# The first panels of a two-layer hybrid kernel: turned rows of x from the host, sums of squares on GpSimd

## What is computed

```python
h = rms_norm(x, g_mix);  proj = h @ w_in               # x: 256 x 1024, w_in: 1024 x 8,000 or so
kv_m = rms_norm(mem, g_mem) @ w_mem_kv                 # mem: 256 x 1024
# rms_norm(t, g) = t * rsqrt(mean(t * t, axis=-1) + 1e-6) * g
```

## Time and profile before

| | |
|---|---|
| median of three runs | 929.32 us (929.22 to 929.41) |
| span of the profiled execution | 926.1 us; the profile gives no other time for that execution |
| TensorE busy | 905.7 us, 98% of the span |
| VectorE, ScalarE, GpSimd busy | 720.6, 534.9, 161.8 us |
| mean granted TensorE clock | 0.997 of full speed |

### The profile page before, as it was taken

How to read it: one execution, slowest core, us unless ns; L and a number is a source line. 1 busy time by engine, 2 the same in 40 slices (tenths; PEclk the granted TensorE clock), 3 DMA queues, 4 the chain that set the end, 5 groups by cost and what they waited for, 6 DMA issues and landing times.

```text
span 926.1 us, 13743 instructions
## 1 busy us (share of the span) xinstructions
PE 905.7 (98%) x4668; PEld 730.1 (79%) x4668; DVE 720.6 (78%) x1030; ACT 534.9 (58%) x831; POOL 161.8 (17%) x247
## 2 busy tenths in 40 slices
PE   8999999999999999999999999999999999999996
PEld 7888888777878778888888887666678788888885
DVE  4779476878777778887679788865668879999976
ACT  6775754476775575555333345656664676666633
POOL 7000000216500000110112001550000023444400
PEclk9999999999999999999999999999999999999998
DMA  9746744876552447887598755322245566555572
GB/s 319 204 150 208 269 138 133 285 263 196 178 191 96 138 141 253 270 266 251 171 358 304 254 159 183 117 78 80 92 131 183 155 191 179 169 176 177 172 251 78
DMA packets 100534, 176.16 MB, mean 190 GB/s; under 512 B 8560, under 2 KB 36592, under 8 KB 100352
## 3 DMA queue, kind: packets, MB, share of 16 engines
q1 hardware_dynamic: 93120, 149.87, 50.7%
q0 software_dynamic: 7184, 25.50, 8.2%
q10 hardware_dynamic: 176, 0.08, 0.0%
HBM read 174.38 MB, written 1.05 MB: 189 GB/s over the span
## 4 chain that ended last, share of the span: by engine, by line
PE 59%; DVE 4%; ACT 2%; issue 1%; DVEq 0%
PE acc L775 50%; PE turned L1251 2%; PE scores L1240 1%; PE turned L867 1%; DVE wlo L1938 1%; PE turned L1353 1%; PE turned L1140 1%; PE turned L1163 1%; PE turned L811 1%; ACT prob L1790 0%; DVE soft L2643 0%; ACT whi L1393 0%; DVE turn L2025 0%; PE turned L1255 0%; ACT turn L1847 0%
## 5 line engine op out<-in xcount | busy, mean ns | idle before, releaser
L1938 DVE TENSOR_TENSOR wlo<-raw,whi 128x1024 fp32r<-128x1024 f32 (+3 forms) x269 | 346.6, 1308 | 81.8 <-ACT whi L1393 71.2
L1393 ACT CAST whi<-raw 128x1024 fp32r<-128x1024 f32 (+3 forms) x269 | 273.3, 1032 | 161.7 <-PE acc L775 118.0
L775 PE MATMUL acc<-whi,lta_hi 128*128 128x512 f32 (+2 forms) x576 | 163.4, 399 | 0.2 <-DVEq L2515 0.2
L775 PE MATMUL acc<-whi,lta_lo 128*128 128x512 f32 (+2 forms) x576 | 155.8, 385 | 0.0
L775 PE MATMUL acc<-wlo,lta_hi 128*128 128x512 f32 (+2 forms) x576 | 155.4, 385 | 0.0
L775 PEld LDWEIGHTS acc<-whi,lta_hi 128*128 128x128 f32 x576 | 101.1, 188 | 30.8 <-issue 10.8
L775 PEld LDWEIGHTS acc<-whi,lta_lo 128*128 128x128 f32 x576 | 106.9, 188 | 22.4
L775 PEld LDWEIGHTS acc<-wlo,lta_hi 128*128 128x128 f32 x576 | 106.9, 188 | 21.9
L657 POOL DMA_DIRECT2D wm<-in_w_mod x48 | 34.4, 719 | 428.6 <-DVEq L2069 245.6
L775 PE MATMUL acc<-whi,ltb_hi 128*128 128x512 f32 (+1 forms) x268 | 73.3, 392 | 1.6 <-ACT ltb_hi L1851 0.8
L775 PE MATMUL acc<-wlo,ltb_hi 128*128 128x512 f32 (+1 forms) x268 | 71.1, 384 | 1.6 <-DVE wlo L1938 1.6
(11 more groups left out here) (371 smaller groups left out, 1301.7 us busy)
## 6 DMA issues: line engine op xcount, KB each, us to landing
raw<-in_w_in SPq DMA_DIRECT2D x88, 512.0 KB, 4.2
wm<-in_w_mod POOLq DMA_DIRECT2D x48, 512.0 KB, 5.5
raw<-in_w_up SPq DMA_DIRECT2D x88, 256.0 KB, 3.1
raw<-in_w_up SPq DMA_DIRECT2D x32, 512.0 KB, 4.6
raw<-in_w_down SPq DMA_DIRECT2D x32, 512.0 KB, 5.2
raw<-in_w_down SPq DMA_DIRECT2D x44, 256.0 KB, 3.0
raw<-in_w_o SPq DMA_DIRECT2D x8, 512.0 KB, 4.5
raw<-in_w_out SPq DMA_DIRECT2D x8, 512.0 KB, 4.6
```

The lines of the kernel that those rows point to most:

```text
L775: ins = pe.matmul(acc[s][:, t, 0:n], lhs[part][:, kt0 + kk, tok], w[:, u % RING, kk, 0:n], start=(opens and k == 0 and kk == 0 and j == 0) ...
L1393: act.copy(whi[:, s, :, 0:n], raw[:, s, :, 0:n]).then_inc(hi_ready, 1)
L1938: dve.tensor_tensor(wlo[:, s, :, 0:n], raw[:, s, :, 0:n], whi[:, s, :, 0:n].bitcast(F32), ALU.subtract)\
```

## The change

The host hands over x turned as well (`x_t`), the eight gains in one array and AQ's two column ranges side by side (`w_aq`). In the kernel:

- SyncE loads a quarter of `xT` behind each unit of MK2. Memory's rows aren't loaded; x's rows (for the residual) follow the first two units of V0.
- `lta` is made of `xT` in SBUF with the gain and without the root. TensorE turns nothing here. ScalarE applies the root of x as it evicts AQ, GQ, CK, GK, V0, V1 and the Q panels, in two instructions in place of one; VectorE does so for R and the gates.
- GpSimd squares `memT` and then `xT`, 512 columns at a time, and adds them up: eight squares, six additions and two last additions of 256 columns. TensorE sums over the partitions with two matmuls of one column for each of the two (`row_sums`), memory's after MK2's first unit, x's after AQ. VectorE's `row_var` and the root follow.
- The first half of unit 0 is cast by VectorE. The table of the root is loaded at the start.

```diff
-    out += [("AQ", KT, 2)]
+    out += [("AQ", KT, 1)]
...
-    out = g("h", 4) + ["aT", "z.0", "z.1", "mqT", "mkT", "ck"]
+    out = ["mem_sum", "x_sum", "aT", "z.0", "z.1", "mqT", "mkT", "ck"]
...
+        feature_squares = [prob[:, 0, 0:SEQ], prob[:, 1, 0:SEQ]]
...
-                return [(0, rows(w, k)[:, :, COL["a"]:COL["a"] + GATE_RANK]),
-                        (GATE_RANK, rows(w, k)[:, :, COL["qm"]:COL["qm"] + 256])]
+                return [(0, a["w_aq"][:, UNIT * k:UNIT * k + UNIT, :])]
...
-                    if name == "MK1" and k == units_of(name) - 1:
-                        for t in range(T):
-                            sp.dma_start(memx[:, t], a["mem"][t * P:(t + 1) * P, :]).then_inc(ev(f"mem{t}_landed"), 16)
-                    if name == "MK2" and k < T:
-                        sp.dma_start(x[:, k], a["x"][k * P:(k + 1) * P, :]).then_inc(ev(f"x{k}_landed"), 16)
+                    if name == "MK2":
+                        sp.dma_start(xT[:, 2 * k:2 * k + 2, :], a["x_t"][:, 2 * k:2 * k + 2, :])\
+                          .then_inc(ev(f"xT{k}_landed"), 16)
+                    if name == "V0" and k < T:
+                        sp.dma_start(x[:, k], a["x"][k * P:(k + 1) * P, :]).then_inc(ev("x_landed"), 16)
...
+            for s, (name, src, landed_as) in enumerate((("mem", memT, "memT"), ("x", xT, "xT"))):
+                total, part = work[:, s, 0:COLS], work[:, s, COLS:D]
+                for g in range(4):
+                    pool.wait_ge(ev(f"{landed_as}{g}_landed"), 16)
+                    v = src[:, 2 * g:2 * g + 2, :].rearrange("p a b -> p (a b)")
+                    order.done(pool.tensor_tensor(part if g else total, v, v, ALU.mult))
+                    if g:
+                        order.done(pool.tensor_tensor(total, total, part, ALU.add))
+                pool.tensor_tensor(feature_squares[s], total[:, 0:SEQ], total[:, SEQ:COLS], ALU.add)\
+                    .then_inc(ev(f"{name}_squares"), 1)
...
-            for name, view in GAIN.items():
-                pool.dma_start(view, a[name].partition_broadcast(P)).then_inc(ev("gains_landed"), 16)
+            pool.dma_start(gains[:], a["gains"].partition_broadcast(P)).then_inc(ev("gains_landed"), 16)
...
+            def row_sums(name, squares):
+                bank, full = t_begin(f"{name}_sum")
+                pe.wait_ge(ev(f"{name}_squares"), 1)
+                for t in range(T):
+                    ins = pe.matmul(bank[:, t:t + 1], squares[:, P * t:P * t + P], one_col[:], start=True, stop=True)
+                ins.then_inc(full, 1)
+
             for k in range(4):
-                if k == 3:
-                    pe.wait_ge(ev("h_scaled"), T)
-                    turn_tokens("h", work, groups=(0, 1))
                 unit("MK2", k, ltb)
-            turn_tokens("h", work, groups=(2, 3))
+                if k == 0:
+                    row_sums("mem", feature_squares[0])
             panel("AQ", lta, NARROW["AQ"], new="h")
+            row_sums("x", feature_squares[1])
...
-            for name, src, s in (("me", memx, 0), ("h", x[:], 1)):
-                for t in range(T):
-                    ...
-                    act.activation(prob[:].rearrange("p a b -> p (a b)"), src[:, t, :], ACT.Square,
-                                   accum_out=stat[:, s, t:t + 1]).then_inc(ev(f"{name}_sum"), 1)
...
+            for g in range(4):
+                ahead(2 + g)
+                lt_act("h", lta, (g,))
+            ahead(PLAN.unit["AQ"] - 2)
+            sqrt("mem", stat[:, 0, 2:4])
...
-            evac("AQ", aq[:], NARROW["AQ"])
+            ahead(last_unit("AQ") + 1)
+            sqrt("x", stat[:, 1, 2:4])
+            normed_rows("AQ", aq, NARROW["AQ"])
...
+            dve.wait_ge(ev("first_landed"), 16)
+            dve.tensor_copy(whi[:, 0, 0], raw[:, 0, 0]).then_inc(ev("first_hi"), 1)
             lt_dve("me", ltb, col("g_mem", 0, 8), between=lambda g: ahead(g - 2), sent=memT)
...
-            for t in range(T):
-                dve.tensor_scalar(work[:, t], x[:, t], stat[:, 1, 2 + t:3 + t], None, ALU.mult)\
-                   .then_inc(ev("h_scaled"), 1)
...
+            for g in range(4):
+                ahead(2 + g)
+                lt_dve("h", lta, col("g_mix", 0, 8), groups=(g,))
+            ahead(PLAN.unit["AQ"] - 2)
+            row_var("mem", 0)
+            inverse("mem", stat[:, 0, 2:4])
+            dve.sem_inc(ev("mem_inverse"), 1)
+            ahead(PLAN.unit["GQ"])
+            row_var("x", 1)
+            inverse("x", stat[:, 1, 2:4])
+            dve.sem_inc(ev("x_inverse"), 1)
+            evacuated("AQ")
```

More of the change, by code:

```diff
@@ L289, in hybrid_kernel @@
         ln_sums = sb("ln_sums", [P, T, 8])
-        gains = sb("gains", [P, 6 * 64 + DV_GLA + HEADS])
+        gains = sb("gains", [P, sum(n for _, n in GAINS)])
         ROWS, at = {}, 0
@@ L584, in _ @@
                     panel(name)
-                if name == "MK2":
+                if name == "AQ":
                     sp.dma_start(ccol[:], a["columns"][:, 96:96 + 8 * FT2].rearrange("p (v r) -> p v r", v=4))\
@@ L1418, in lt_act @@
                     if name in LT_DIRECT:
-                        if name == "me":
-                            act.wait_ge(ev(f"memT{g}_landed"), 16)
+                        if name in LT_HOST:
+                            act.wait_ge(ev(f"{'memT' if name == 'me' else 'xT'}{g}_landed"), 16)
                         else:
@@ L1531, in _, with normed_rows @@
             normed_memory("MK1", kvm[:, :, 256:768], COLS)
[L1532 to L1535, removed]
             normed_memory("MK2", kvm[:, :, 768:1280], COLS)
-            evac("AQ", aq[:], NARROW["AQ"])
+            ahead(last_unit("AQ") + 1)
+            sqrt("x", stat[:, 1, 2:4])
+            def normed_rows(name, dst, n=COLS):
+                ahead(last_unit(name) + 1)
+                panel_wait(name)
+                if name == "AQ":
+                    act.wait_ge(ev("x_inverse"), 1)
+                s, _ = PLAN.bank(name)
+                for t in range(T):
+                    ins = act.activation(dst[:, t], acc[s][:, t, 0:n], ACT.Copy, scale=stat[:, 1, 2 + t:3 + t])
+                ins.then_inc(panel_out[s], 1)
+            normed_rows("AQ", aq, NARROW["AQ"])
             act.dma_start(wg[0:GATE_RANK, :], a["w_gla_gate"]).then_inc(ev("wg_landed"), 16)
@@ L1581, in mem_after @@
                         act.wait_ge(panel_out[b], k + 2)
-                    act.activation(rsig, acc[PLAN.bank(name)[0]][:], ACT.Sigmoid).then_inc(ev("r_sig"), 1)
+                    for t in range(T):
+                        ins = act.activation(rsig[:, t], acc[PLAN.bank(name)[0]][:, t], ACT.Sigmoid,
+                                             scale=stat[:, 1, 2 + t:3 + t])
+                    ins.then_inc(ev("r_sig"), 1)
                     if i == 1:
@@ L2319, in mem_after @@
                     v = r_gla[:, :, c:c + COLS]
-                    frees(name, dve.tensor_tensor(v, p[:], rsig, ALU.mult))
+                    for t in range(T):
+                        ins = dve.scalar_tensor_tensor(v[:, t], p[:, t], stat[:, 1, 2 + t:3 + t], rsig[:, t], ALU.mult, ALU.mult)
+                    frees(name, ins)
                     for t in range(T):
@@ L2332, in gate_in_psum @@
                 dve.wait_ge(bias_landed[n % 2], 16 * (n // 2 + 1))
-                dve.tensor_tensor(p[:], p[:], bias[:, n % 2].unsqueeze(1).broadcast_to([P, T, COLS]), ALU.add)\
-                   .then_inc(gate_in, 1)
+                for t in range(T):
+                    ins = dve.scalar_tensor_tensor(p[:, t], p[:, t], stat[:, 1, 2 + t:3 + t], bias[:, n % 2],
+                                                   ALU.mult, ALU.add)
+                ins.then_inc(gate_in, 1)
                 dve.wait_ge(gate_in, n + 1)
@@ L2897, in laid_out @@
     arrays = {f"in_{name}": np.ascontiguousarray(inputs[name]) for name in _INS}
+    arrays["in_gains"] = np.ascontiguousarray(np.concatenate([np.asarray(inputs[name]).reshape(-1) for name, _ in GAINS]))
+    w = np.asarray(inputs["w_in"]).reshape(KT, P, -1)
+    aq = np.concatenate([w[:, :, COL["a"]:COL["a"] + GATE_RANK], w[:, :, COL["qm"]:COL["qm"] + 256]], axis=2)
+    arrays["in_w_aq"] = np.ascontiguousarray(aq.transpose(1, 0, 2))
     conv = np.asarray(inputs["conv_w_2"]).reshape(3, 2 * FF2)
@@ L2901, in laid_out @@
         + [in_columns(inputs[name]) for name in ("conv_b_2", "ln1_g_2", "ln1_b_2")], axis=1))
-    arrays["in_mem_t"], arrays["in_ctx_t"] = turned_tokens(inputs["mem"]), turned_tokens(inputs["ctx_2"])
+    for name in ("x", "mem"):
+        arrays[f"in_{name}_t"] = turned_tokens(inputs[name])
+    arrays["in_ctx_t"] = turned_tokens(inputs["ctx_2"])
     return arrays
```

76 lines of the change are left out of this document (28 added, 48 removed).

## The result

The changed kernel takes 938.44 us (median of 4 runs, 937.03 to 939.46) against 929.27 us before (929.19 to 929.41): a ratio of 1.0095, with an interval of 1.0078 to 1.0112. It is slower, as forecast, by 9.2 us where 6.2 were forecast. That lies inside the stated range of 928 to 940, and just past the 933 to 938 that the prediction gave its own mechanism.

A forecast was written before the change was run, and what follows sets the result against it. TensorE, busy for 98% of the span, was taken as the bound. Span 926.1 + 5.9 (GpSimd and VectorE excluding each other) + 0.3 (V0's loads) = 932.3; median 929.3 + 6.2 = 935.5 us, range 928 to 940.

The forecast's parts named there:

- What is removed: MK1 to AQ: turns of x, waits around them and MK2's gaps go; GQ 3.2 us earlier if nothing else happened.
- The row sums: TensorE, memory's and x's sums: a pair of one-column matmuls costs 0.24 to 0.5 us, taken as 0.25 each.
- The exclusion: First panels: GpSimd's squares and additions alternate with VectorE's two-SBUF-input instructions, low parts included, each waiting for the other's end.
- The walk: From 6.2 us to GQ, engine by engine with strict alternation: AQ at 39.2, GQ at 45.4, 5.9 us later.
- MK1's eviction as the last wait: Ahead of AQ: memory's mean, root, reciprocal and MK1's eviction stand behind `wlo` 8, so AQ begins at 39.2.
- x's rows in V0: 1 MB of x's rows between V0's loads makes a later load pass through to TensorE: 0.3 us taken.
- a hole of about one transfer: Load queue around V0: a gap that takes in x's rows, leaving 0 to 1.4 us of cost, 0.3 taken.
- The stretches after V0: ScalarE's evictions in two instructions, 1.3 us in place of 1.03: nothing, or up to 0.5 us where TensorE waits.
- The time around the span: Difference between median and profiled span, taken as 3.2 us and fixed.
- The squares hide: Rival, first panels: GpSimd doesn't hold up the low parts, or gives way; 926.4 us, chance 0.19.
- VectorE goes first: Rival, first panels: GpSimd starves, memory's row sums become the wait; 1.3 to 3.6 us later, 931 to 933, chance 0.15.
- TensorE's clock: Rival, first panels: waits drop the clock from 2.4 to 1.2 GHz for two units; 941 us, chance 0.05.

The follow-up runs named there:

- e3: Changed kernel with constants in place of GpSimd's squares and sums, and x's rows loaded behind R1 in place of V0; 926.72 us, 0.9993 of the kernel before.
- e4: Changed kernel with each GpSimd square and addition replaced by a memset that reads nothing, sums constant; 929.49 us, 1.0023 of the kernel before.
- e1: Changed kernel without GpSimd's squares and sums, constants in their place, x's rows still in V0; 928.99 us, 1.0019 of the kernel before.
- e9: As e5, but memory's mean, root and reciprocal follow VectorE's unit 7 subtraction, MK1's eviction ahead of unit 8's cast; 929.33 us, 1.0007 of before.
- e5: Changed kernel with the squares on ScalarE, only additions on GpSimd, x's rows behind R1; 928.91 us, 1.0012 of the kernel before.
- e6: As e5, but memory's mean, root, reciprocal and MK1's eviction ahead of unit 7's split; 930.42 us, 1.0026 of the kernel before.
- e8: Changed kernel, GpSimd's squares kept, x's rows behind R1, memory's root chain and MK1's eviction ahead of unit 7's split; 938.31 us, 1.0111 of before.
- e2: Changed kernel with the two transfers of x's rows behind R1's units in place of V0's; 935.57 us, 1.0094 of the kernel before.
- e7: The changed kernel run again, unedited, on the chip of later runs; 937.74 us, 1.0106 of the kernel before.
- e10: As e9, but ScalarE squares x after MK2's eviction and AQ's casts, x's row sums behind GQ's second unit; 930.70 us, 1.0027 of before.

## Why the prediction was right, point by point

- **What is removed.** Forecast: 3.2 us of lead at GQ if nothing else happened. e3 shows 3.16 and e4 3.24. Shown. The row sums cost 0.36 us for a pair (26.74 to 27.10 in the trace after), where 0.25 was taken out of 0.24 to 0.5.
- **The exclusion.** Forecast: GpSimd's operations and VectorE's with two SBUF inputs, the low parts among them, take turns. Right, and shown by e1 and e4 together: the lengths go back to those alone when memsets stand in for the squares and additions, with GpSimd busy still. That it is the reading of SBUF that decides fits these runs but isn't parted by them from the arithmetic. The Trainium skill ("SBUF — State Buffer", section "SBUF: two separate sides") has the lock against "a GpSimd op that reads SBUF" alone; e4's 1.22 us beside memsets of 0.96 us agrees with that too. The masks' selects, which read SBUF, show one side of it only: they wait for VectorE, and beside them its subtraction grows from 1.22 to 1.28 us at most (at 31.96 in the trace after).
- **The walk.** Units 1 to 7 were to start at 12.7, 18.0, 21.3, 24.0, 26.9, 30.1 and 34.4; they started at 13.14, 16.93, 21.23, 24.01, 27.10, 30.84 and 34.35. `wlo` 1 ended at 15.84, 1.2 us earlier than in the walk: GpSimd waited 0.24 us for memory's second quarter (to 7.68), and a low part went through without a turn of GpSimd's. Unit 2 was 1.1 us early by it and unit 6 0.7 late; the other five agree to 0.5 us. `wlo` 8 ended at 36.68 (forecast 36.9), AQ began at 38.75 (39.2), GQ at 45.27 (45.4). Of the 5.9 us forecast at GQ, 5.8 were measured. That this is so close is partly luck: AQ came 0.45 us earlier than forecast, and took 6.52 us to GQ where the forecast has 6.2.
- **MK1's eviction as the last wait.** Right by the order of time. e9 confirms the mechanism: with the chain 1.5 us earlier than in e5 (the eviction at 29.71 in place of 31.20), AQ comes 0.9 us earlier, and then waits for its own first cast. e6 and e8 show that it can't simply be moved up, because the casts behind it are next.
- **x's rows in V0: the term that was mis-sized.** The prediction took 0.3 us, "0 to 1.4 us", for "a hole of about one transfer". In the traces V0 and what leads to it cost 2.45 us with the squares (5.8 late at GQ, 8.25 behind V0) against 0.04 in e2 (5.52 and 5.56), where the rows stand elsewhere. Without the squares it is 1.8 in e1 against 0.6 in e3. From V0's second unit to the scores behind V0 alone, the four traces with the rows in V0 lose 2.2 (after, e7), 2.1 (e4) and 1.7 us (e1), and the seven with the rows behind R1 lose 0.3 at most. The working looked at one late load alone; but the rows delay three loads, VectorE then enters its chain of norms late, and the next subtraction stands behind all of that chain.
- **The stretches after V0** were priced at nothing, with up to 0.5 us for evictions in two instructions. They cost 2.3 us in the profiled execution (8.25 to 10.5), 1.4 in e2 and 1.7 in e3. Three steps are the same in every version, at 206.6, 311.6 and 536.65 us of the trace before: 0.17, 0.17 and 0.39 us. The second comes after a gate to which VectorE now applies the root in two instructions, 1.41 us together, in place of one of 1.23. The step at the turns of `x_res` at 721.94 is another matter: 1.15 us in the profiled execution, where TensorE waits 0.99 us, 0.35 in e7, which is the same kernel, and 0.03 in e5. So most of it differs from one execution to the next. What the other steps belong to, the changed order of loads or the changed evictions, wasn't tried and stays open.
- **The time around the span** was taken as 3.2 us and fixed. It was 1.8 in the changed kernel (938.44 to 936.6); in the experiments it was 1.8 to 1.9 in the versions of the changed kernel and 1.6 in the kernel before, so 0.2 us of the loss lies there. If the kernel before took 1.6 in its profiled execution too, which no run shows, that execution was about 1.6 us under its median (an estimate). On the span the forecast of 932.3 was 4.3 us short, and on the median 2.9: the 3.2 us carried over hid a part of what was missing, by luck.
- **The rivals.** *The squares hide* fell: five waits for `wlo` in the first panels, of 3.3 us together. *VectorE goes first* fell: GpSimd got every second turn, and memory's row sums made no wait. *TensorE's clock* did fall, for unit 0 alone, and at GQ it cost at most 0.3 us (below).

So the 10.5 us between the two profiled spans are 9.0 for the squares (5.8 late at GQ, where the kernel would have been 3.2 early), less those 3.2, and 2.4 for V0 and 2.3 for the rest, of which the last is open.

## What to carry to other kernels

Ask of each instruction that is moved to an idle engine what it shares with the busy one: seventeen microseconds of squares and additions on an idle GpSimd cost nine here, while fourteen microseconds of memsets were free. A walk, engine by engine with turns at the shared resource, found five of seven starts to half a microsecond and the other two to 1.1; the terms that were priced by a glance (a load in a hole of the queue) were those that failed. And where a chain of small instructions ends last, look at what is queued behind it before moving it up: in e6, e8 and e10 the wait only passed to the next cast or subtraction, and the 1.0 us that e9 won at GQ was gone by V0.

## What the runs showed of the hardware

The granted clock fell in the first unit. In the kernel after it is 0.52 from 9.50 to 12.80 us (the row above), after TensorE, behind late low parts, had been busy for 1.72 of the 3.5 us from 6.0 to 9.5. Through the fall it was nearly always busy (3.19 of 3.30 us), and full clock was back when unit 1 began. In e7 it fell earlier, after 0.70 busy of the 2.0 us from 6.0 to 8.0; in e8, with 1.48 busy of the same 2.0, it didn't fall at all. The stretches of e7, and then of e8 (length, busy time of PE, granted clock, DMA share, GB/s):

```profile
8.00:9.50 1.50, 1.37 (x3) 0.53 1.01 345
9.50:10.60 1.10, 1.10 (x4) 0.50 1.06 406
```
```profile
8.00:9.50 1.50, 1.36 (x5) 1.00 1.00 344
9.50:10.60 1.10, 1.10 (x6) 1.00 1.05 397
```

At 1.2 GHz two matmuls take 1.05 us in place of 0.62. Yet the matmuls that wait for `wlo` 1 start at 15.03 in e7 and in e8 alike: the fall lay in the shadow of VectorE's wait. e2 is the same program up to V0 and had no fall either; its GQ starts at 44.99, that of e7 at 44.97. In the first profiled execution GQ starts at 45.27, 0.3 us after e2's: the fall can have cost that at most, if the two executions were alike otherwise.
